# A two-layer trunk step on one core: the gate projections of two branches by Strassen's scheme

## The chip, the cores and the metric

The kernel runs on one core of one Trainium2 chip. The metric is the device time of one execution in microseconds (us), the median of several runs. Everything is 32-bit floating point. A core has TensorE for matmuls (PE in the profile, with PEld for its weight loads), VectorE (DVE), ScalarE (ACT), GpSimd (POOL), and SyncE (SP), which here only issues DMA transfers.

## The reference

Two layers run one after the other over 640 tokens: 512 latent tokens of a sample and 128 context tokens of a prompt. What matters here of each layer is this:

```python
h = rmsnorm(x, lw['g_norm1']) * (1.0 + sc1) + sh1
(qa, ka, va, qb, kb, vb, zb, ab, bb, qc, kc, vc, ga, gb, gc) = split_cols(h @ lw['w_in'])
...
merged = (jax.nn.sigmoid(ga) * (oa @ lw['w_br_a'])
          + jax.nn.sigmoid(gb) * (ob @ lw['w_br_b'])
          + jax.nn.sigmoid(gc) * (oc @ lw['w_br_c']))
x = x + gt1 * (merged @ lw['w_out'])
h2 = rmsnorm(x, lw['g_norm2']) * (1.0 + sc2) + sh2
x = x + gt2 * expert_choice_ffn(h2, lw['w_router'], lw['w_e_gate'], lw['w_e_up'], lw['w_e_down'])
```

`h` is 640 x 1024. The queries, keys and values `qa` to `vc` are 512 wide each; the gates `ga`, `gb`, `gc` are 1024 wide each. The shifts, scales and gates `sh1` to `gt2` come from a product of the condition with `w_ada` (1024 x 6144). Branch a is differential attention, branch b a bidirectional gated DeltaNet over five tiles of 128 tokens, branch c neighbourhood attention. The feed-forward part has 16 experts.

## The kernel before, in words

Weights stream from HBM in chunks of 2 MB (1024 rows by 512 columns) through a ring of three SBUF slots, `ring`, in the order of the list `PLAN`. SyncE loads a chunk when the chunk that had its slot has been used. `h` lies turned in `hT`, features on the partitions, as 8 blocks of 640 tokens. A chunk of `w_in` gives 512 output columns in five units. A unit is one PSUM bank of 512 columns, and two banks, `unit0` and `unit1`, alternate: TensorE may begin unit n when ScalarE has emptied unit n-2 (`begin`, waiting on `unit_emptied`). For a chunk with features on the partitions (`fill_rows`) the first unit holds the prompt tokens (32 matmuls of 128 columns, L988) and the other four hold 128 features by 512 sample tokens each (8 matmuls of 512 columns, L997). `fill_tokens` does it for `va` and `vc` (L1009). ScalarE copies a unit into one of eight stage buffers in `xT`, whose content lies in HBM meanwhile, and SyncE stores it to `spill`; when a branch needs it, SyncE loads it back. Four of the units of `qa` and of `ka` are rotated by VectorE before GpSimd stores them.

Each layer begins with four condition chunks (`ada`) and the chunks `qb`, `kb`, `vb`, `zb` of the DeltaNet branch. The DeltaNet is a chain of small products on TensorE with VectorE and ScalarE between them. TensorE fills the time of this chain with other work: the generator `filler` gives the matmuls of all chunks in `FILL` (condition chunks 4 to 11, `va`, `kc`, `qc`, `vc`, `qa`, `ka`, `ga` twice, `gb` twice), and `fill(gap)` takes a fixed number of calls from it at each place of the table `GAPS`: ("kv", 3) and ("kv", 4) beside the last keys and values, ("pp", t) beside the key products, "inverse" beside VectorE's inversion, (p, 0) to (p, 5) in the five rounds p of the state recurrence, and ("o", h) beside the turning of its output. A call is one matmul of 512 columns or four of 128. ScalarE's `drain(gap)` empties the units that end in a gap, in the same order. A condition chunk is two calls; behind every fourth one stands a `fold`, four small matmuls on what ScalarE has copied from the sum of the four chunks.

The gaps of one round are bounded by these lines of TensorE: L1171 (state products, behind the gap of the round before), L1179 and L1185 (behind gap 0), L1194 three times (behind gaps 1, 2 and 3), L1200 and L1204 (behind gap 4). After the five rounds come gap ("o", 4), four times L1214 and L1215 with the other ("o", h), L1134 and L1137 (turning keys), and then attention (L1242, L1254 and on). The third gate `gc` is computed beside attention (`late_units`, L1025 and L1028). Its two chunks are loaded behind `gb`. At the end of the recurrence ScalarE squares the output (`square_out`, L1780), takes roots (L1799), and only then drains ("o", 4). GpSimd issues small loads: tiles of the inversion (L779), the rotated stores (L804), caches (L814, L815) and attention biases (L828), which it then masks (L849, L854).

Of the kernel before, what the change touches and what calls it, by code (L numbers as in the profile page):

```python
# [28 lines left out]
P = 128  # L29
# [7 lines left out]
H = 4  # L37
# [28 lines left out]
UNITS_OF = dict(ada=0, fm=5, tm=5, br=5, late=0)  # L66
LATE = [("gc", 0), ("gc", 1)]
BRANCHES = "bca"
FILL = []
_a = 4  # L70
for _s in [("va", 0), ("kc", 0), ("qc", 0), ("vc", 0), ("qa", 0), ("ka", 0)] + [("g" + b, i) for b in "ab" for i in (0, 1)]:
    if _a < 12:
        FILL += [("ada", _a), _s] + [("fold", _a)] * (_a % 4 == 3)
        _a += 1
    else:
        FILL += [_s]
SPILLED = [_f for _f in FILL if _f[0] not in ("ada", "fold")]
PLAN = [("ada", a) for a in range(4)] + [("qb", 0), ("kb", 0), ("vb", 0), ("zb", 0)]
# [4 lines left out]
def kind_of(name):  # L83
    return "ada" if name == "ada" else "late" if name == "gc" else "tm" if name in ("va", "vc") else "br" if name.startswith("br") else "fm"
# [33 lines left out]
MSLOTS = (0, 3, 1, 2, 4, 5)  # L118
MRING = len(MSLOTS)
assert PRE_CHUNKS % RING == 0 and NMOE % MRING == 0  # L120


def slot_of(c):

    l, q = c // LAYER_CHUNKS, c % LAYER_CHUNKS
    if q < PRE_CHUNKS:
        return q % RING, l * (PRE_CHUNKS // RING + NMOE // MRING) + q // RING + 1
    s, n = MSLOTS[(q - PRE_CHUNKS) % MRING], (q - PRE_CHUNKS) // MRING + 1
    if s >= RING:
        return s, l * (NMOE // MRING) + n  # L130
    return s, (l + 1) * (PRE_CHUNKS // RING) + l * (NMOE // MRING) + n


def slot_before(c):

    l, q = c // LAYER_CHUNKS, c % LAYER_CHUNKS
    if q < RING:
        return l * LAYER_CHUNKS - MRING + MSLOTS.index(q)
    if q < PRE_CHUNKS:
        return c - RING  # L140
    if q < PRE_CHUNKS + MRING:
        return l * LAYER_CHUNKS + PRE_CHUNKS - RING + MSLOTS[q - PRE_CHUNKS]
    return c - MRING
# [87 lines left out]
STEPS = (9, 8, 8, 8, 8, 8)  # L231
GAPS = {("kv", 3): 3, ("kv", 4): 3} | {("pp", _t): 11 for _t in range(5)} | {"inverse": 90}
GAPS |= {(_i, _j): _q for _i in range(5) for _j, _q in enumerate(STEPS)}
GAPS |= {("o", _h): 8 if _h == 4 else 3 for _h in (4, 0, 1, 2, 3)}


def fill_units():

    units = []
    for name, i in FILL:  # L240
        if name == "ada":
            units.append((name, i, 0, 2))
        elif name == "fold":
            units.append((name, i, 0, 1))
        else:
            units += [(name, i, j, 8) for j in range(5)]
    return units
# [2401 lines left out]
```

## Time and profile before

| | us |
|---|---|
| median of 3 runs (3076.04 to 3077.58) | 3077.04 |
| the profiled execution's own time | 3078.97 |
| its span, first to last instruction | 3077.1 |
| TensorE busy, of the span | 3011.0 |
| VectorE busy | 1239.2 |
| ScalarE busy | 603.7 |
| GpSimd busy | 234.4 |

The granted TensorE clock was 0.993 of full speed over the span. The profiled execution took 1.9 us longer than the median and its span is 1.9 us shorter than its own time. A layer's part before its experts takes about 1000 us in the first layer (0 to 1000) and in the second (from about 1500). The experts take the rest. [...]

### The profile page before, as it was taken

The numbers are of one execution on the slowest core, as the hardware profiler recorded it, in microseconds if no ns is written. First come the engines' busy times: TensorE is split into PE (matmuls) and PEld (weight loads), VectorE is DVE, ScalarE is ACT, GpSimd is POOL, SyncE is SP. The second block draws the span as 40 slices with busy tenths as digits, with TensorE's granted clock in tenths as the row PEclk, the third lists the DMA queues.
The fourth block names the chain that finished last, engine by engine and source line by source line (L and its number), as shares of the span: only waits on it lengthen the run. The fifth ranks groups of instructions, "written<-read, shape, count | busy, mean of one in ns | idle before, by whom it ended". The sixth has DMA issues, their size and how long they took to land.

```text
span 3077.1 us, 49446 instructions
## 1 busy us (share of the span) xinstructions
PE 3011.0 (98%) x21834; PEld 1601.7 (52%) x21834; DVE 1239.2 (40%) x2404; ACT 603.7 (20%) x1349; POOL 234.4 (8%) x374
## 2 busy tenths in 40 slices
PE   7999999999999999999999999999999989999998
PEld 3555565656555444444455546666565454444443
DVE  4459553365354121221254694532644342112113
ACT  3241001144423000000032400011534230000001
POOL 0011000021001000000100100000110010000000
PEclk9999999999999999999999999999999989999999
DMA  6235432432343999999941552434224349999996
GB/s 269 97 130 191 155 146 97 140 123 74 133 157 125 408 398 397 403 399 396 373 176 55 187 199 93 151 118 144 93 74 145 142 174 410 395 405 400 395 403 269
DMA packets 102294, 695.55 MB, mean 226 GB/s; under 512 B 11786, under 2 KB 25142, under 8 KB 66752
## 3 DMA queue, kind: packets, MB, share of 16 engines
q1 hardware_dynamic: 75296, 613.97, 50.6%
q0 software_dynamic: 20736, 62.80, 7.0%
q10 hardware_dynamic: 6048, 15.62, 1.4%
q8 instruction: 172, 2.82, 0.4%
q14 instruction: 42, 0.34, 0.0%
HBM read 618.66 MB, written 73.68 MB: 225 GB/s over the span
## 4 chain that ended last, share of the span: by engine, by line
PE 95%; ACT 3%; DMA 1%; DVE 1%; issue 1%; DVEq 0%; POOLq 0%
PE unit L1523 14%; PE unit L997 14%; PE unit L951 12%; PE work L1526 11%; PE work L1523 7%; PE unit L1009 4%; PE unit L988 4%; PE unit L1028 4%; PE unit L1381 4%; PE unit L941 3%; PE work L965 1%; PE work L1171 1%; PE work L1194 1%; PE unit L1025 1%; DMA ring<-in_w_ada 1%; PE work L1488 1%
## 5 line engine op out<-in xcount | busy, mean ns | idle before, releaser
L997 PE MATMUL unit<-hT,ring 128*128 128x512 f32 x1024 | 452.6, 594 | 0.0
L997 PEld LDWEIGHTS unit<-hT,ring 128*128 128x128 f32 x1024 | 189.4, 190 | 217.7 <-issue 217.7
L2548 DVE SCALAR_TENSOR_TENSOR arena<-work,arena 32x256 f32<-32x256 f32 x128 | 61.7, 482 | 533.5 <-PE work L1526 532.1
L1523 PE MATMUL unit<-ring,arena 128*32 128x512 f32 x2112 | 243.4, 602 | 3.3 <-DVE arena L2536 3.3
L951 PE MATMUL unit<-hT,ring 128*128 128x512 f32 x512 | 222.2, 593 | 0.0
L1526 PE MATMUL work<-ring,arena 128*32 128x256 f32 x3072 | 183.8, 380 | 2.4 <-DVE arena L2536 2.4
L2018 ACT ACTIVATE arena<-work 128x512 f32<-128x512 f32 x32 | 19.1, 597 | 822.4 <-PE work L1541 822.4
L1629 ACT ACTIVATE xT<-unit 128x512 f32<-128x512 f32 x92 | 54.8, 596 | 590.7 <-PE unit L997 384.8
L951 PE MATMUL unit<-arena,ring 128*128 128x512 f32 x384 | 167.9, 593 | 1.6 <-ACT arena L1629 0.9
L951 PEld LDWEIGHTS unit<-hT,ring 128*128 128x128 f32 x512 | 96.2, 190 | 115.7 <-issue 115.5
L1523 PEld LDWEIGHTS unit<-ring,arena 128*32 128x32 f32 x2112 | 69.9, 111 | 149.1 <-issue 143.3
L1526 PEld LDWEIGHTS work<-ring,arena 128*32 128x32 f32 x3072 | 97.2, 110 | 92.2 <-issue 39.6
L1009 PE MATMUL unit<-ring,hT 128*128 128x512 f32 x320 | 140.7, 594 | 0.0
L988 PEld LDWEIGHTS unit<-hT,ring 128*128 128x128 f32 x1024 | 116.8, 192 | 12.4 <-issue 12.4
L1526 PE MATMUL work<-arena 128*32 128x256 f32 x2048 | 122.3, 379 | 0.0
L988 PE MATMUL unit<-hT,ring 128*128 128x128 f32 x1024 | 121.2, 277 | 0.0
L951 PEld LDWEIGHTS unit<-arena,ring 128*128 128x128 f32 x384 | 71.7, 190 | 89.1 <-issue 84.2
L1523 PE MATMUL work<-arena 128*32 128x512 f32 x1024 | 115.8, 592 | 2.1 <-ACT arena L2019 2.1
L1028 PE MATMUL unit<-hT,ring 128*128 128x512 f32 x256 | 117.0, 600 | 0.0
L2275 DVE TENSOR_TENSOR arena<-arena,work 32x512 f32<-32x512 f32 x60 | 41.0, 683 | 186.9 <-PE work L1194 186.5
L1523 PE MATMUL unit<-arena 128*32 128x512 f32 x1024 | 115.7, 592 | 0.0
L904 POOL DMA_INDIRECT moe_sum<-arena,slotu x30 | 43.2, 1440 | 941.7 <-DVE arena L2553 941.7
(447 smaller groups left out, 4201.0 us busy)
## 6 DMA issues: line engine op xcount, KB each, us to landing
ring<-in_w_e_up SPq DMA_DIRECT2D x64, 2048.0 KB, 18.5
ring<-in_w_in SPq DMA_DIRECT2D x32, 2048.0 KB, 11.6
arena<-in_w_e_gate SPq DMA_DIRECT2D x32, 2048.0 KB, 17.0
arena<-in_w_e_down SPq DMA_DIRECT2D x32, 2048.0 KB, 19.6
xT<-in_w_e_gate SPq DMA_DIRECT2D x30, 2048.0 KB, 17.1
ring<-in_w_e_down SPq DMA_DIRECT2D x30, 2048.0 KB, 17.5
ring<-in_w_ada SPq DMA_DIRECT2D x24, 2048.0 KB, 9.5
spill<-xT SPq DMA_DIRECT2D x94, 256.0 KB, 9.9
```

The costliest lines, as they stand in the source:

```text
L904: pool.indirect_dma_start(moesum[l], bass.IndirectOffsetOnAxis(token[:, s:s + 1], 0), Y[s % NROWS][0:SL, :], None, compute_op=ALU.add)\
L941: last = mm(bank[:, tile_t(m)], w[:, k, m * P:(m + 1) * P], src[:, k, TS:T], start=k == 0, stop=k == kk - 1)
L951: last = mm(bank[:, :], w[:, k, m * P:(m + 1) * P], src[:, k, 0:TS], start=k == 0, stop=k == kk - 1)
L988: last = mm(bank[:, tile_t(m)], w[:, k, m * P:(m + 1) * P], hT[:, k, TS:T], start=k == 0, stop=k == KD - 1)
L997: last = mm(bank[:, :], w[:, k, m * P:(m + 1) * P], hT[:, k, 0:TS], start=k == 0, stop=k == KD - 1)
L1009: last = mm(big[:, :], hT[:, k, tile_t(t)], w[:, k, :], start=k == 0, stop=k == KD - 1)
L1028: last = mm(ps[1][:, :], w[:, s, (j - 1) * P:j * P], hT[:, s, 0:TS], start=s == 0, stop=s == KD - 1)
L1381: last = mm(bank[:, :], wo[half][:, k, m * P:(m + 1) * P], merged[:, k, 0:TS], start=k == 0, stop=k == KD - 1)
L1523: last = mm(big[SLOTP * c:SLOTP * c + SLOTP, :], x[:, s0:s0 + SLOTP], w[:, kk, 512 * (c // 2):512 * (c // 2) + 512], start=k == 0, stop=k ...
L1526: last = mm(low[SLOTP * c:SLOTP * c + SLOTP, 0:256], xp, w[:, kk, 256 * c:256 * c + 256], start=k == 0, stop=k == KD - 1)
L1629: emptied(a_(dst, unit(n)[:, :], f, scale=scale))
L2548: STT(y[SLS:SLS + SLOTP, 256 * c:256 * c + 256], W[5][r, 0:256], gpro[r, e:e + 1], gatep[r, :], ALU.mult, ALU.mult)
```

## The change

The chunks `ga` and `gb` become a kind of their own, `fast`. In a chunk (1024 x 512), two output tiles of 128 columns, j and j+2, are one pair: the weights are a 2 x 2 of blocks A11, A12, A21, A22 (128 columns by half of the 1024 rows), and `hT` is a 2 x 2 of blocks B11, B12, B21, B22 (half of the rows by half of the 640 tokens). The four output blocks, 128 x 320 each, come from seven block products of four matmuls with 320 columns, in seven units (`fill_fast`). GpSimd makes the sums of blocks of weights before them, of `hT` once for each layer (T2, T3, T4 in ring slot 2, T1 over B12 in place), and the sums of products afterwards (`fast_sums`). ScalarE copies each product into one of two sets or a spare buffer (`copy_fast`), and SyncE stores a whole pair at once (`store_pair`). B12 is stored to HBM beforehand and loaded back when the last product that uses T1 is done, and TensorE waits for it before the late gate (`h_restored`).

The order of the fills is another one: `FILL` begins with two condition chunks, `kc` comes last of the plain ones, `vc` behind the fold of chunk 7, and each fold directly behind its condition chunk. Calls are now counted in eighths, 8 for a plain call and 5 for a matmul of 320 columns, and the credit of a gap is 8 times its number in `GAPS`. The last `gc` chunk is loaded behind `gb`, and `va` is loaded back before the last pair is stored.

```diff
+FAST = [("ga", 0), ("ga", 1), ("gb", 0), ("gb", 1)]
+FILL = [("ada", 4), ("ada", 5), ("va", 0), ("ada", 6), ("qc", 0), ("ada", 7), ("fold", 7), ("vc", 0), ("ada", 8), ("qa", 0),
+        ("ada", 9), ("ka", 0), ("ada", 10), ("kc", 0), ("ada", 11), ("fold", 11)] + FAST
-STEPS = (9, 8, 8, 8, 8, 8)
+STEPS = (8, 7, 7, 7, 8, 8)
-GAPS |= {("o", _h): 8 if _h == 4 else 3 for _h in (4, 0, 1, 2, 3)}
+GAPS |= {("o", _h): 10 if _h == 4 else 3 for _h in (4, 0, 1, 2, 3)}
...
+            if r == 1:
+                out += [("s4", g)]
+            if r == 2:
+                out += [("u2", g), ("c11", g)]
+            if r == 3 and g + 1 < NPAIRS:
+                out += [("s1", g + 1), ("s2", g + 1), ("s3", g + 1)]
+            if r == 4:
+                out += [("u3", g)]
+            if r == 5:
+                out += [("c12a", g), ("c12", g), ("c22", g)]
+            if r == 6:
+                out += [("c21", g)]
...
                 back(flat(K[0]), "ka", 0, "k_loaded")
                 back(flat(Q[0]), "qa", 0, "q_loaded")
-                store_plan(last)
+                store_pair(NPAIRS - 2)
                 sp.wait_ge(sig["q_loaded"], 16 * (2 * l + 1))
                 sp.wait_ge(sig["k_loaded"], 16 * (2 * l + 1))
                 back(flat(aV), "va", 0, "v_loaded")
+                sp.wait_ge(sig["unit_computed"], fast_unit(l, NPAIRS - 1, 3) + 1)
+                sp.dma_start(B12, hsave).then_inc(sig["h_restored"], 16)
+                load_plan(FIRST_LATE + 1)
+                store_pair(NPAIRS - 1)
...
+                    def add(out, x, y, op, task):
+                        pool.tensor_tensor(out, x, y, op).then_inc(sig["summed"], 1)
+
+                    for kind, g in TASKS[gap]:
+                        pool.wait_ge(sig["summed"], task_done(l, kind, g) - 1)
...
+                    for r, (x, y, need) in enumerate((
+                            (A11, B11, None), (A12, B21, None), (S2, T2, "s2"), (S1, B12, "s1"), (A21, T3, "s3"), (A12, B22, "s4"),
+                            (A22, T4, "t4"))):
+                        n = unit_no(l, name, i, 7 * j + r)
+                        bank = begin(n)
+                        if need and (g == 0 or need != "t4"):
+                            pe.wait_ge(sig["summed"], task_done(l, need, g))
+                        if g == 0 and r == 3:
+                            pe.wait_ge(sig["summed"], task_done(l, "t1", 0))
+                        for k in range(4):
+                            last = mm(bank[:, 0:TH], x[:, k, :], y[:, k, :], start=k == 0, stop=k == 3)
...
+                    if r == 0 and g >= 2:
+                        act.wait_ge(sig[f"stage{g % 2}_stored"], 16 * (l * STORES[g % 2] + STAGED[g % 2] + g // 2))
...
+                    elif g and r in (1, 2, 4):
+                        act.wait_ge(sig["summed"], task_done(l, {1: "c11", 2: "c12a", 4: "c21"}[r], g - 1))
```

TensorE beside the last keys and values (L1092 and, with the new line numbers, L1264), before:

```order
L1092 MATMUL work<-cst,arena 128x128 x12
L965 MATMUL work<-ring,ccol 8x512 x8
L1009 MATMUL unit0<-ring,hT 128x512
L1092 MATMUL work<-cst,arena 128x128 x12
L1009 MATMUL unit0<-ring,hT 128x512 x3
```

and now (L1113 is a condition chunk, L1157 the values `va`):

```order
L1264 MATMUL work<-cst,arena 128x128 x12
L1113 MATMUL work<-ring,ccol 8x512 x12
L1264 MATMUL work<-cst,arena 128x128 x12
L1113 MATMUL work<-ring,ccol 8x512 x4
L1157 MATMUL unit0<-ring,hT 128x512 x2
```

Half of chunk 5 has come before the second L1264 and half behind it, and `va`, whose slot is free only when `zb` is done, begins directly behind.

TensorE in round 2 at the first fast chunk (L1366 was L1194; L1113 and L1122 are condition chunk 11 and its fold; L1179 is now the product of 320 columns):

```order
L1113 MATMUL work<-ring,ccol 8x512 x4
L1366 MATMUL work<-arena 32x128 x8
L1113 MATMUL work<-ring,ccol 8x512 x4
L1122 MATMUL work<-cst,xT 128x8 x4
L1179 MATMUL unit0<-hT,ring 128x320 x4
L1179 MATMUL unit1<-hT,ring 128x320 x4
L1366 MATMUL work<-arena 32x128 x8
L1179 MATMUL unit0<-ring,xT 128x320 x4
L1179 MATMUL unit1<-hT,xT 128x320 x4
```

Two products stand between the fold and the first one that needs sums (`ring,xT`: T2 and S2).

GpSimd at the end of the recurrence (L874 is a sum, L959 and L960 were L814 and L815, L973 was L828), before only the DMAs, now:

```order
L874 TENSOR_TENSOR xT<-xT 128x320
L959 DMA arena<-in_cache_diff_k 128x512
L960 DMA arena<-in_cache_diff_v 128x512
L874 TENSOR_TENSOR xT<-xT 128x320 x4
L874 TENSOR_TENSOR ring<-ring,xT 128x4x128
L959 DMA arena<-in_cache_na_k 128x512
L960 DMA arena<-in_cache_na_v 128x512
L874 TENSOR_TENSOR xT<-xT 128x320 x7
L973 DMA arena<-rpb_scratch 16x8x32 x16
```

Five sums stand between the two cache loads and seven before the bias loads.

## Rows read from the trace of the kernel before

**Rows 1.** Page: busy us by engine, and TensorE's share in 40 slices.

```profile
PE 3011.0 (98%) x21834; PEld 1601.7 (52%) x21834; DVE 1239.2 (40%) x2404; ACT 603.7 (20%) x1349; POOL 234.4 (8%) x374
PE   7999999999999999999999999999999989999998
```

**Rows 2.** Stretches: length, busy us and instructions by engine, clock, DMA share, GB/s.

```profile
400.00:500.00 100.00, 100.00 (x548) 60.41 (x547) 49.39 (x103) 8.94 (x15) 8.04 (x15) 1.00 0.37 137
1200.00:1300.00 100.00, 100.00 (x1214) 41.29 (x1210) 19.87 (x42) 5.23 (x12) 7.06 (x6) 1.00 1.01 400
```

**Rows 3.** Groups by shape, instructions as in the page's part 5.

```profile
L1526 PE MATMUL work<-xT,arena 128*32 128x256 f32 x1024 | 61.9, 382 | 0.0
L988 PE MATMUL unit<-hT,ring 128*128 128x128 f32 x1024 | 121.2, 277 | 0.0
L997 PE MATMUL unit<-hT,ring 128*128 128x512 f32 x1024 | 452.6, 594 | 0.0
```

**Rows 4.** Stretches as rows 2, of L988, then of L997, alone.

```profile
502.70:509.00 6.30, 6.25 (x56) 6.28 (x56) 1.00 1.00 353
...
605.80:619.70 13.90, 13.82 (x32) 5.97 (x32) 1.00 0.88 301
```

**Rows 5.** Timeline of TensorE at the end of `zb`: start, length, instructions.

```profile
183.63 1.47 PE L1092 MATMUL work<-cst,arena 128*128 128x128 f32 x12
185.03 1.90 PE L965 MATMUL work<-ring,ccol 128*8 128x512 f32 x16
189.41 2.74 PE L1009 MATMUL unit<-ring,hT 128*128 128x512 f32 x6
192.58 1.16 PE L1150 MATMUL work<-arena 128*128 128x128 f32 x8 [0.43 <-ACT work L1737]
```

**Rows 6.** Timeline of SP's load behind `zb`, and its landing time.

```profile
183.82 0.33 SPq L582 DMA_DIRECT2D ring<-in_w_ada  x1
...
ring<-in_w_ada SPq DMA_DIRECT2D x1, 2048.0 KB, 7.9
```

**Rows 7.** Waits of TensorE: us in total, times, longest us.

```profile
PE work L974 <- ACT arena L1634: 0.7, 1, 0.7
PE work L965 <- ACT mod L1638: 0.8, 2, 0.4
```

**Rows 8.** GpSimd's sums of two SBUF operands: ns min/median/max.

```profile
L875 POOL TENSOR_TENSOR xT<-xT,arena x4: 1267/1270/1272, 971.9 to 2512.2; 128x512 f32<-128x512 f32 x4
L854 POOL TENSOR_TENSOR arena<-arena,cst x32: 407/417/471, 635.7 to 2280.5; 128x128 f32<-128x128 f32 x32
L849 POOL TENSOR_TENSOR arena<-arena,cst x32: 295/308/767, 635.1 to 2281.2; 128x64 f32<-128x64 f32 x32
```

**Rows 9.** Timeline of round 3 of the recurrence, VectorE and TensorE.

```profile
502.32 0.69 DVE L2257 TENSOR_TENSOR arena<-arena 128x512 f32<-128x512 f32 x1
502.93 1.28 DVE L2260 TENSOR_TENSOR arena<-work,sc 128x512 f32<-128x512 f32 x2
510.72 1.95 PE L1179 MATMUL work<-arena 128*128 128x128 f32 x16
```

**Rows 10.** Timeline of ScalarE, then of TensorE, at the recurrence's end.

```profile
611.29 0.60 ACT L1629 ACTIVATE xT<-unit 128x512 f32<-128x512 f32 x1 [9.85 <-PE unit L997]
615.16 0.22 ACT L1799 ACTIVATE sc<-sc 128x20 f32<-128x20 f32 x1
644.59 0.60 ACT L1882 ACTIVATE xT<-unit 128x512 f32<-128x512 f32 x1 [1.14 <-PE unit L1025]
...
604.09 1.95 PE L1204 MATMUL work<-arena 128*128 128x128 f32 x16
605.88 13.90 PE L997 MATMUL unit<-hT,ring 128*128 128x512 f32 x32
637.06 7.41 PE L1025 MATMUL unit<-hT,ring 128*128 128x128 f32 x64
```

**Rows 11.** Page, DMA issues: SP's stores of units, median us to landing.

```profile
spill<-xT SPq DMA_DIRECT2D x94, 256.0 KB, 9.9
```

More of the change, by code:

```diff
@@ L241, in fill_units @@
         if name == "ada":
-            units.append((name, i, 0, 2))
+            units.append((name, i, 0, 2, 8))
         elif name == "fold":
-            units.append((name, i, 0, 1))
+            units.append((name, i, 0, 1, 8))
+        elif kind_of(name) == "fast":
+            units += [(name, i, j, 4, 5) for j in range(14)]
         else:
-            units += [(name, i, j, 8) for j in range(5)]
+            units += [(name, i, j, 8, 8) for j in range(5)]
     return units
 def drains():
-    at, left, out = iter(fill_units()), 0, {}
-    unit = next(at)
-    left = unit[3]
+    pieces = [(u[:3] if k == u[3] - 1 else None, u[4]) for u in fill_units() for k in range(u[3])]
+    at, credit, out, calls = 0, 0, {}, {}
     for gap, n in GAPS.items():
-        out[gap] = []
-        for _ in range(n):
-            if unit is None:
-                break
-            left -= 1
-            if left == 0:
-                out[gap].append(unit[:3])
-                unit = next(at, None)
-                left = unit[3] if unit else 0
-    out["rest"] = ([unit[:3]] if unit else []) + [u[:3] for u in at]
-    return out
-DRAINS = drains()
+        credit, begin = credit + 8 * n, at
+        while at < len(pieces) and pieces[at][1] <= credit:
+            credit -= pieces[at][1]
+            at += 1
+        out[gap], calls[gap] = [u for u, _ in pieces[begin:at] if u], at - begin
+    out["rest"] = [u for u, _ in pieces[at:] if u]
+    return out, calls
+DRAINS, CALLS = drains()
 ROTATED = [(_n, _j) for _n in ("qa", "ka") for _j in range(1, 5)]
@@ L856, in mask_bias @@
                                     .then_inc(sig["bias_ready"], 1)
+                for h in range(H):
+                    fast_sums(("o", h))
+                fast_sums("rest")
                 load_bias(0)
@@ L1049, in filler @@
                         yield from fill_tokens(l, name, i)
+                    elif kind_of(name) == "fast":
+                        yield from fill_fast(l, name, i)
                     else:
@@ L1126, in fill @@
                 def fill(gap):
-                    for _ in range(GAPS[gap]):
+                    for _ in range(CALLS[gap]):
                         next(fills, None)
```

232 lines of the change are left out of this document (183 added, 49 removed).

## The prediction

> **What bounds the kernel now.** I read the page first: TensorE is busy in 98% of the span, and 37 of its 40 slices stand at 9 [rows 1]. Then the stretches: in 400 to 500 us, inside the recurrence, it is busy all the time at a granted clock of 1.00, VectorE half of it and GpSimd 8 us of 100; among the experts (1200 to 1300) TensorE and the DMA engines are both full [rows 2]. So work taken from TensorE before the experts is worth its full length unless a wait takes its place. The experts begin earlier by as much and last as long as before. Then I read the shapes, to price a matmul, and last the places where an instruction of the new order is followed by what waits for it.
>
> **What the products cost.** The length of an instruction with 128 rows of weights grows in a straight line: 277 ns for 128 columns, 594 ns for 512, and between them 382 ns for 256 [rows 3] (the line gives 383; that row has narrower weights). So 320 columns lie on the line. What an instruction takes from the engine is less than its length, since they overlap: 6.25 us for 56 of L988 is 0.112 us each, 13.82 us for 32 of L997 is 0.432 us each [rows 4]. The line between these gives 0.272 us for 320; I take 0.271. Bounds: it is not cheaper than 320/512 of 0.432, which is 0.270, and not dearer than 0.432.
>
> A gate chunk has 32 matmuls of 128 and 32 of 512 columns, which are 64 instructions of each: 64 x 0.112 + 64 x 0.432 = 34.8 us. Now it has two pairs of seven products of four matmuls, 112 instructions: 112 x 0.271 = 30.4 us. That is 4.4 us less for each chunk, and there are four in each of two layers: 35 us less. The other fills are the same matmuls in another order.
>
> **GpSimd's sums.** A sum of 512 columns takes 1.27 us and one of 128 takes 0.42 us [rows 8], so 2.2 ns for each further column: 0.84 us for 320 and 3.0 us for 1280. A pair needs four of 512 and seven of 320: 11.0 us, about 12 with the hand-over between chained sums, estimated at 0.1 us each (the wait of 0.7 us in [rows 7] is one copy of 0.60 us, as long as L1629's [rows 10], and 0.1 us of hand-over). TensorE needs 56 x 0.271 = 15.2 us for a pair if nothing stands between, and the recurrence does: in the trace of before the gates' place, from about 465 us to the end of the fills near 635, is 170 us; less 18 for the saving it is 152 for eight pairs, 19 us each. So GpSimd is free a third of the time, and its sums are hidden by the products.
>
> The first pair has the least room. After the last unit of `kc`, GpSimd does T3, T2, S1, S2 (3.0 + 3.0 + 1.3 + 1.3 = 8.6 us, 9.0 with hand-overs) before the third product. TensorE has a condition chunk (1.9 us [rows 5]), a fold, two products (4.3 us) and two steps of the recurrence: about 9 us with the fold's wait. T1, S3, T4 and S4 (8.5 us more) meet products four to six with as little room. I take 0.5 us a layer, with bounds 0 and 4, since one sum that is late moves all behind it.
>
> **What the shorter gaps uncover.** The gaps of a round go from 49 calls to 45, which is 3.4 us less, and no gap loses more than one call of 0.86 us. The chain behind L1171 ends on VectorE at 504.2, and TensorE comes for it at 510.7 [rows 9]: 6.5 us of room, of which the gap takes 0.9. The other steps of a round have as much, so I take nothing. The SBUF page of the Trainium skill (SBUF — State Buffer, Who interferes with whom) says that a GpSimd instruction that reads SBUF and a VectorE instruction with two SBUF inputs shut each other out for a whole instruction. That speaks against this change, and is weighed among the rivals.
>
> **What the new order costs.** (1) The slot of `va` is free when `zb` ends, at 183.8. The load at that place, of another 2 MB chunk, landed after 7.9 us [rows 6], which is 191.7. In the new order TensorE arrives at the values after two condition chunks (1.9 us each from 185.03) and one turning (1.4 us), at 190.2, and needs two calls, 1.8 us, before the key products. So these start at about 193.6 and not at 192.6, where TensorE also had waited 0.43 us [rows 5]: 1.0 us a layer; bounds 0 and 3.
> (2) A fold directly behind its chunk waits for ScalarE's copy. This occurs once in the trace, at the head of the kernel: 0.7 us [rows 7]. Two folds a layer do so now: 1.4 us a layer. The wait of the chunk behind a fold, 0.4 us and once a layer [rows 7], goes. Together 1.0 us a layer.
> (3) In gap ("o", 4) ScalarE squares and takes roots first; between its drain at 611.29 and the end of the root at 615.38 are 4.1 us [rows 10]. Two units of 3.5 us hid it. Units now last 2.2 us. Counted from 605.88, the last unit of (4, 5) ends at 6.5, ScalarE is free at 11.1, has emptied the next at 11.6, and TensorE wants that bank at 10.8: 0.8 us a layer.
> (4) The late gate needs B12 back. Its load is issued at about 21 us on the same count and TensorE asks at 31 (L1025 starts at 637.06) [rows 10]. A read of 640 KB has 10 us: nothing. `va` loaded earlier gives nothing, since it was not waited for.
> (5) The last pair: its final sum ends 2.5 us behind the last product, and its store then stands behind the 2 MB of `gc`, issued when the last product ends. With 7.9 us for that load and 1.5 for the store's own 640 KB it lands 9.5 us after the fills. ScalarE copied the first late unit at 644.59, 9.7 us after the fills [rows 10], and may now not until that store has landed. I take 0.5 us a layer, bounds 0 and 3.
> (6) Twice as many units want a prompt ScalarE (a bank must be empty after 2.2 us and not 3.5 to 7), also while it waits for sums or stores: 0.7 us a layer, bounds 0 and 6.
>
> Sum for a layer: 17.5 - 0.5 - 1.0 - 1.0 - 0.8 - 0.5 - 0.7 = 13.0 us, and 26 us for both. Against the profiled execution this is 3079.0 - 26 = 3053 us. That execution took 1.9 us longer than the median, so for the median: 3077 - 26 = **3051 us**. Without any wait it would be 3042; with all the bounds at their far ends at once the waits are 2 x 18 us and the time 3078.
>
> **Rivals.**
> A. The banks. If each fast unit ended up waiting for ScalarE, which waits in order for sums (units 1, 2 and 4 of a pair), for the store of the pair before the last (unit 0) and for its own part of the recurrence, the cost is (6) at its end and (5) with it: a store took 9.9 us to land [rows 11], mostly behind a 2 MB load, and two of them in a layer that miss by 3 us give 3051 + 12 = 3063 us. For it: ScalarE had one drain for 7 us of TensorE and now has one for 2.2. Against: by my count the store of pair 5 has some 6 us of room before pair 7.
> B. GpSimd becomes the pace. If each of its 11 sums of a pair waits for one VectorE instruction of 0.69 us [rows 9], a pair takes 12 + 7.6 = 19.6 us against 19, in the dense stretch behind round 4 against 15 to 17; with the first pair's chain late by four of them (2.8 us) this is some 5 us a layer, 3061 us. [...] For B: one of L849's sums took 767 ns against a median of 308 [rows 8]. Against: VectorE is busy half the time and less in rounds 3 and 4, and much of that reads PSUM.
> C. Slower than before. The same contention, with GpSimd's sums taking 1.7 times their priced length or more. A pair of 12 us may grow to 19 unnoticed. Beyond that each microsecond costs 8 in a layer; the gain of 13 us a layer is gone at 20.6 us a pair. At the ratio of that worst row, 767 to 308, a pair takes 27 to 30 us, and the kernel is slower by 8 x 2 x 9 less 26, about 120 us; at twice the length, 24 us a pair, it is slower by 54: 3131 us. It decides at 1.7. Against: L875 and L854 hold their lengths within 5 and 64 ns over 36 instructions.
> D. The saving isn't there: 320 columns cost more than the line says. At 0.309 us an instruction a chunk costs 34.6 us again, and the kernel would be at about 3086. The row of 256 columns, on the line within a nanosecond, speaks against it.
>
> **How the numbers follow.** Forecast 65% (3043 to 3058), A 15%, B 11%, C 5%, D 2%, and 2% for something not seen. The range is 3042 to 3067: it takes the floor without waits, the forecast's own, A and B. A run can hardly tell less than 0.2% here, 6 us. Faster by more than that (under 3070.9) in the forecast, in A and B nearly always: 0.89. Within it: the tails of A and B and the gentle part of C, 0.05. Slower: C and D, 0.06.
>
> **What would show it.** The product's row should have 896 instructions (8 chunks of 112) with a length of 434 ns, and 0.27 us from one to the next. L997 and L988 should have half their counts. TensorE's wait for the first chunk of `va` should be 1 to 2 us in each layer, and each fold's 0.7. GpSimd should be busy some 200 us more, its sums 1.27, 0.84 and 3.0 us long. Waits of the products for sums beyond 2 us a layer would speak for B, waits for ScalarE's emptying beyond 2 us a layer for A. The forecast is wrong if the span shrinks by less than 15 or more than 35 us, or if a stretch among the experts changes its length.

## The result and the profile after

The changed kernel takes 3051.11 us (median of 4 runs, 3049.69 to 3054.68), beside 3077.31 us for the kernel before on the same chip: a ratio of 0.9914, 95% interval 0.9900 to 0.9929. That is 26.2 us less. The forecast was 3051, with a range of 3042 to 3067. Two later sets of runs of the same kernel gave 3050.77 and 3049.83 us.

Where a line of before has moved, the new number is given with it. The page of the changed kernel, busy us by engine and TensorE's slices [rows 1]:

```profile
PE 2976.9 (98%) x21706; PEld 1615.5 (53%) x21706; DVE 1260.3 (41%) x2404; ACT 628.3 (21%) x1421; POOL 444.3 (15%) x558
PE   7999999999998999999999999999999989999998
```

TensorE has 128 instructions fewer and is busy for 34.1 us less. The span shrank by 24.2 us, so 10 us more of it is idle; most of that is the new waits below. GpSimd is busy for 210 us more, VectorE for 21. The same stretches as in [rows 2] (length, busy us and instructions of PE, PEld, DVE, ACT, POOL, clock, DMA share, GB/s):

```profile
400.00:500.00 100.00, 99.22 (x549) 66.54 (x548) 47.39 (x87) 11.26 (x23) 42.69 (x38) 1.00 0.32 115
1200.00:1300.00 100.00, 100.00 (x1222) 41.55 (x1215) 19.89 (x42) 5.23 (x12) 7.98 (x7) 1.00 1.01 401
```

The experts are as they were. In the recurrence one wait of 0.78 us has come in, and GpSimd is busy for 43% and not 8%. The products and the sums by shape (duration in ns, min/median/max), which answer to [rows 3] and [rows 8]:

```profile
L1179 PE MATMUL unit<-hT,ring x384: 432/432/537, 460.1 to 2131.6; 128*128 128x320 f32 x192
L1179 PE MATMUL unit<-ring x256: 432/432/537, 470.0 to 2133.7; 128*128 128x320 f32 x128
L874 POOL TENSOR_TENSOR xT<-xT x112: 849/859/1410, 473.1 to 2136.4; 128x320 f32<-128x320 f32 x112
L874 POOL TENSOR_TENSOR xT<-xT,ring x16: 1262/1266/1600, 463.2 to 2109.5; 128x512 f32<-128x512 f32 x16
L874 POOL TENSOR_TENSOR ring<-ring,hT x2: 2876/2878/2879, 458.9 to 1972.7; 128x1280 f32<-128x1280 f32 x2
```

With the two forms not shown (128 of `ring,xT`, 128 of `hT,xT`) these are 896 instructions of products, two for each of the 8 chunks' 56 matmuls. How far one stands from the next is read from the timeline of TensorE in pair 1, whose products follow each other directly:

```profile
473.34 2.32 PE L1179 MATMUL unit<-hT,ring 128*128 128x320 f32 x8
475.49 2.32 PE L1179 MATMUL unit<-ring 128*128 128x320 f32 x8
477.64 2.32 PE L1179 MATMUL unit<-hT,ring 128*128 128x320 f32 x8
```

Eight take 2.15 us from start to start, 0.269 us each, against 0.271 forecast. The waits of TensorE (us in total, times, longest us) in the whole run, those that are new or have grown:

```profile
PE work L1652 <- DMA arena<-h_rows,slotu: 3.3, 2, 1.6
PE work L1122 <- ACT xT L1807: 3.1, 4, 0.8
PE work L1386 <- DVE arena L2502: 2.4, 2, 1.2
...
PE unit L1157 <- DMA ring<-in_w_in: 2.3, 2, 1.2
```

L1157 (before L1009) and L1122 (before L974, [rows 7]) are the waits of terms (1) and (2). L1386 and L1652 were not in the prediction. No row names a product that waits for GpSimd.

Because a kernel's instructions on TensorE stand in a fixed order, the start of the same instruction in two runs says what has been won up to there. Starts in the changed kernel less those in the kernel before, us (each is the first instruction of its line in the stretch, read from the two timelines; the last two rows are the group of products that ends the experts' turns, before and behind it):

| place (line before) | layer 1 | layer 2 |
|---|---|---|
| last keys and values (L1092) | +0.4 | -10.9 |
| key products (L1150) | +1.3 | -10.0 |
| round 0 (L1171) | +2.1 | -9.2 |
| round 1 | -2.1 | -13.3 |
| round 2 | -5.5 | -16.7 |
| round 3 | -9.4 | -20.6 |
| round 4 | -13.2 | -24.5 |
| norm (L1214) | -13.3 | -24.5 |
| attention (L1242) | -14.5 | -25.7 |
| first expert (L1479) | -12.8 | -26.2 |
| expert turns, all 16 | -12.2 | -25.7 |
| behind the last expert | -10.7 | -24.2 |

From its own start up to attention layer 1 gains 14.5 us and layer 2 15.0 (2.1 us are lost up to round 0 of layer 1 and the rest won behind it). The experts take as long as before, to 0.01 us over all 16. But 3.8 us are given back between attention and the next layer in layer 1, and 1.5 in layer 2. Of this, 1.5 us in each layer is one group of products behind the last turn. The kernel before, then the changed one (start, length), and the changed one's clock there (the third value from the end):

```profile
1517.20 3.64 PE L1523 MATMUL work<-arena 128*32 128x512 f32 x32 [1.05 <-ACT arena L2019]
```
```profile
1505.04 5.12 PE L1696 MATMUL work<-arena 128*32 128x512 f32 x32 [1.05 <-ACT arena L2214]
```
```profile
1504.00:1508.00 4.00, 2.96 (x16) 0.92 (x20) 0.00 (x0) 0.87 (x2) 4.00 (x9) 0.58 0.96 339
```

The granted clock fell to about half there, and at 3020 us again. In layer 1, 1.6 us more are the wait L1652 for the first gathered rows.

### The profile page after: what moved, and what is told of

Read it like the earlier page. It is cut to its first block, busy times and chain, and to the rows that moved or that the text cites. A ratio compares the mean times of both kernels' runs of the same rounds, so it can differ in the third digit from the quotient of the medians.

```text
span 3052.9 us, 49631 instructions
## 1 busy us (share of the span) xinstructions
PE 2976.9 (98%) x21706; PEld 1615.5 (53%) x21706; DVE 1260.3 (41%) x2404; ACT 628.3 (21%) x1421; POOL 444.3 (15%) x558
## 4 chain that ended last, share of the span: by engine, by line
PE 94%; ACT 2%; DMA 2%; DVE 1%; issue 1%; ACTq 0%; DVEq 0%; POOLq 0%
PE unit L1696 14%; PE unit L1099 12%; PE work L1699 11%; PE unit L1179 7%; PE work L1696 7%; PE unit L1145 7%; PE unit L1157 5%; PE unit L1198 4%; PE unit L1554 4%; PE unit L1089 3%; PE unit L1136 2%; PE work L1343 1%; PE work L1113 1%; PE work L1366 1%; PE unit L1195 1%; DMA ring<-in_w_ada 1%
## 5 line engine op out<-in xcount | busy, mean ns | idle before, releaser
L1145 PE MATMUL unit<-hT,ring 128*128 128x512 f32 x512 | 225.3, 593 | 0.0
L1099 PE MATMUL unit<-hT,ring 128*128 128x512 f32 x512 | 222.2, 592 | 0.0
L1099 PE MATMUL unit<-arena,ring 128*128 128x512 f32 x384 | 167.9, 593 | 1.6 <-ACT arena L1802 0.9
L1099 PEld LDWEIGHTS unit<-hT,ring 128*128 128x128 f32 x512 | 96.2, 190 | 115.8 <-issue 115.5
L1145 PEld LDWEIGHTS unit<-hT,ring 128*128 128x128 f32 x512 | 95.0, 190 | 109.3 <-issue 109.3
L1157 PE MATMUL unit<-ring,hT 128*128 128x512 f32 x320 | 139.7, 593 | 2.3 <-DMA ring<-in_w_in 2.3
L1198 PE MATMUL unit<-hT,ring 128*128 128x512 f32 x256 | 117.0, 600 | 0.0
L1179 PE MATMUL unit<-hT,ring 128*128 128x320 f32 x384 | 111.6, 435 | 0.2
L874 POOL TENSOR_TENSOR xT<-xT 128x320 f32<-128x320 f32 x112 | 101.7, 908 | 62.5 <-ACT xT L1875 56.4
L1554 PE MATMUL unit<-arena,ring 128*128 128x512 f32 x256 | 110.7, 593 | 0.0
L1696 PE MATMUL work<-ring,arena 128*32 128x512 f32 x960 | 108.5, 592 | 0.0
```

The source lines that it names most:

```text
L874: pool.tensor_tensor(out, x, y, op).then_inc(sig["summed"], 1)
L1099: last = mm(bank[:, :], w[:, k, m * P:(m + 1) * P], src[:, k, 0:TS], start=k == 0, stop=k == kk - 1)
L1145: last = mm(bank[:, :], w[:, k, m * P:(m + 1) * P], hT[:, k, 0:TS], start=k == 0, stop=k == KD - 1)
L1157: last = mm(big[:, :], hT[:, k, tile_t(t)], w[:, k, :], start=k == 0, stop=k == KD - 1)
L1179: last = mm(bank[:, 0:TH], x[:, k, :], y[:, k, :], start=k == 0, stop=k == 3)
L1198: last = mm(ps[1][:, :], w[:, s, (j - 1) * P:j * P], hT[:, s, 0:TS], start=s == 0, stop=s == KD - 1)
```

## The experiments

Medians in us; each ratio is against the kernel before in the same set of runs.

| run | median (range) | ratio, 95% interval |
|---|---|---|
| changed_again | 3050.77 (3049.97 to 3052.7) | 0.9907 (0.9892 to 0.9922) |
| order_alone | 3082.15 (3081.01 to 3083.89) | 1.0010 (1.0001 to 1.0019) |
| sums_8_columns | 3046.3 (3045.43 to 3048.7) | 0.9893 (0.9877 to 0.9908) |
| sums_twice | 3144.22 (3141.3 to 3145.9) | 1.0212 (1.0196 to 1.0227) |
| four_sums_twice | 3057.99 (3055.28 to 3061.46) | 0.9929 (0.9915 to 0.9942) |
| folds_later | 3054.33 (3051.83 to 3055.22) | 0.9917 (0.9904 to 0.9931) |
| sums_after_norm | 3044.64 (3043.94 to 3045.39) | 0.9886 (0.9871 to 0.9902) |
| folds_and_sums | 3047.6 (3044.25 to 3048.68) | 0.9897 (0.9882 to 0.9913) |
| norm_repeat | 3046.29 (3043.61 to 3048.15) | 0.9889 (0.9873 to 0.9906) |
| fold7_and_norm | 3045.4 (3041.85 to 3047.09) | 0.9885 (0.9869 to 0.9902) |
| changed_third | 3049.83 (3048.27 to 3051.84) | 0.9903 (0.9887 to 0.9920) |

**The changed kernel again** (no edit).

> The changed kernel once more, beside the others on one chip. Theory (products shorter by an eighth, waits of 4 to 5 us a layer given back): 26 us under the kernel before. Rival (part of the gain is chance of the run): under 20 or over 32. In the profile of the changed kernel one group at the end of each layer's experts took 5.1 us where it took 3.6 before; if that is a matter of the run and not of the change, it is missing or elsewhere in this one.

It repeats the first result within 0.4 us, and the rows L1122, L1157 and L1386 within 0.3 us. The table of starts is the same to 0.5 us up to attention of layer 1. Behind it the two profiles differ by where the clock falls: here the long group behind the experts stands in layer 2 alone, and two others have come in, at 950 and 2462 us (below).

**The order of the fills alone.** The kernel before, with the changed kernel's list and plain gate chunks.

```diff
-FILL = []
-_a = 4
-for _s in [("va", 0), ("kc", 0), ("qc", 0), ("vc", 0), ("qa", 0), ("ka", 0)] + [("g" + b, i) for b in "ab" for i in (0, 1)]:
...
+FILL = [("ada", 4), ("ada", 5), ("va", 0), ("ada", 6), ("qc", 0), ("ada", 7), ("fold", 7), ("vc", 0), ("ada", 8), ("qa", 0),
+        ("ada", 9), ("ka", 0), ("ada", 10), ("kc", 0), ("ada", 11), ("fold", 11), ("ga", 0), ("ga", 1), ("gb", 0), ("gb", 1)]
```

> The kernel before with the new order of the fills (two condition chunks first, folds directly behind their chunks, kc last) and plain gates; no Strassen products. Theory: the order costs by itself what the trace of the changed kernel shows at these places, a wait of 1.1 us for the first va chunk (of which 0.4 us was there before in another wait) and two folds with 0.8 us, less the 0.4 us wait that goes: some 2 us a layer, 4 us slower than before (3081). Then the products alone gave about 30 us. Rival (the order pays for itself by steadier loads, and the products gave only 20): 5 us faster than before.

It loses 2.4 us in the median against 3079.73, where 4 had been expected, and its profiled span is 3.3 us longer. Its waits:

```profile
PE work L968 <- ACT xT L1628: 3.1, 4, 0.8
PE unit L1003 <- DMA ring<-in_w_in: 2.5, 2, 1.3
```

These are the rows L1122 and L1157 of the changed kernel, to 0.2 us: both waits belong to the order of the fills and not to the products. Attention starts 1.6 us late in layer 1, and 14.5 us early in the changed kernel. So the products with all that belongs to them bring 16.1 us up to there, and over the whole run 31.4 us by the medians of this set (3082.15 less 3050.77).

**Sums of 8 columns.** GpSimd adds 8 columns and not 320 to 1280; what the products are made from and give is wrong for the rest.

```diff
+                        out, x, y = [v[:, :, 0:2] if len(v.shape) == 3 else v[:, 0:8] for v in (out, x, y)]
                         pool.tensor_tensor(out, x, y, op).then_inc(sig["summed"], 1)
```

> The changed kernel with each of GpSimd's sums cut to 8 columns, so that the output is not the reference's: what remains of the sums is their order and their waits. Theory (the sums are hidden, except where they lock VectorE out at the norm of the recurrence's output): 2 to 3 us faster than the changed kernel, since the wait of 1.2 us a layer behind the norm goes; VectorE's lines with two SBUF operands fall back to 0.69 us. Rival (GpSimd sets the pace, rival B of the prediction): 8 us faster or more.

The starts of L1171 differ from those of changed_again by 0.14 or 0.15 us in all ten rounds, and by the same in each. Before the end of round 4, nothing is won by sums of almost no length: they are hidden entirely. Behind it TensorE's first product with the norm (L1386) starts 1.4 us earlier in each layer, because its wait is gone. That is 2.8 us; the median is 4.5 us lower, more than the 2 to 3 expected. The mean granted clock of the profiled execution, 0.993 against 0.992, goes that way. This points to VectorE's norm, L2502 (L2307 before, L2503 here). First the kernel before, then the changed kernel, then this one (durations in ns, min/median/max):

```profile
L2307 DVE TENSOR_TENSOR arena<-arena,sc x10: 681/682/691, 615.7 to 2143.2; 128x512 f32<-128x512 f32 x10
```
```profile
L2502 DVE TENSOR_TENSOR arena<-arena,sc x10: 693/1345/1354, 600.5 to 2118.7; 128x512 f32<-128x512 f32 x10
```
```profile
L2503 DVE TENSOR_TENSOR arena<-arena,sc x10: 682/683/693, 600.1 to 2114.6; 128x512 f32<-128x512 f32 x10
```

And the place itself in the changed kernel, VectorE, then GpSimd, then TensorE (start, length):

```profile
600.51 5.77 DVE L2502 TENSOR_TENSOR arena<-arena,sc 128x512 f32<-128x512 f32 x5
...
600.64 5.08 POOL L874 TENSOR_TENSOR xT<-xT 128x320 f32<-128x320 f32 x4 [0.31 <-ACT xT L1875]
605.80 1.60 POOL L874 TENSOR_TENSOR ring<-ring,xT 128x512 f32<-128x512 f32 x1
...
606.33 0.65 PE L1386 MATMUL work<-cst,arena 128*128 128x128 f32 x4 [1.22 <-DVE arena L2502]
```

Four sums and five norm products, all with both operands in SBUF, take turns: 4 x 0.86 + 3.1 is 6.5 us of work apart, and together they end after about 5.8. In the steady turn a sum and a product start every 1.27 us; alone, sums start every 0.93 us and products every 0.62, which makes 1.55. So each holds the other up for most of its length, though not all. The four sums took 1.19 to 1.28 us each and not 0.86, and the products 1.22 in the mean and not 0.69. VectorE's L2486, of the same 512 columns but with one input in PSUM, kept its 680 ns in the recurrence beside the sums (676 to 681, against 672 to 680 before). The Trainium skill (SBUF — State Buffer, Who interferes with whom) says that a VectorE instruction with two SBUF inputs contends with a GpSimd instruction that reads SBUF, for ports held by an exclusive lock, and that one with at most one SBUF input, outside its 2-port modes, does not. For the norm and for L2486 the trace agrees.

The norm isn't the only line that the sums slow. In the recurrence L2490 (L2295 before), both inputs in SBUF, took up to 1948 ns where 692 was the longest before, and a VectorE copy inside SBUF, with one input, took up to 1333. The copy in the kernel before, in the changed one and in this one:

```profile
L2221 DVE COPY arena<-arena x8: 216/217/223, 484.1 to 541.8; 32x128 f32<-32x128 f32 x8
```
```profile
L2416 DVE COPY arena<-arena x8: 215/575/1333, 475.4 to 529.2; 32x128 f32<-32x128 f32 x8
```
```profile
L2417 DVE COPY arena<-arena x8: 214/218/223, 475.0 to 528.8; 32x128 f32<-32x128 f32 x8
```

No row of TensorE's waits names these lines, and the starts of the rounds show that they cost nothing.

**All sums of a pair twice.** Each sum but T1 to T4 is made twice. S3, S4 and sums behind the products stand in place, so the values of the gates are others.

```diff
-                        pool.tensor_tensor(out, x, y, op).then_inc(sig["summed"], 1)
+                        if kind[0] != "t":
+                            pool.tensor_tensor(out, x, y, op).then_inc(sig["summed"], 1)
+                            pool.wait_ge(sig["summed"], task_done(l, kind, g) - 1)
+                            pool.tensor_tensor(out, x, y, op).then_inc(sig["summed"], 1)
+                        else:
+                            pool.tensor_tensor(out, x, y, op).then_inc(sig["summed"], 2)
...
```

> The changed kernel with each of GpSimd's sums but T1 to T4 done twice, one after the other, so that the output is not the reference's. A pair's sums then take about 24.5 us, and TensorE has 20 us for a pair. Theory (they are hidden up to a pair's time and set the pace beyond it, the point at which rival C of the prediction decides): 4.5 x 8 x 2 = 72 us and a few more for the first pair, 70 to 85 us slower than the changed kernel, so some 50 us slower than before. Rival (each sum only delays its own product and most have room): under 20 us slower than the changed kernel.

This is rival C made real. It is 64.5 us slower than the kernel before, where the rival's price for 24 us a pair was 54, and 93 us slower than the changed kernel, beyond the 70 to 85 expected. TensorE's waits:

```profile
PE unit L1184 <- POOL ring L877: 47.4, 16, 5.6
...
PE unit L1184 <- ACT xT L1880: 12.4, 10, 3.3
```

In layer 1 round 3 starts 5.5 us late against the changed kernel, round 4 19, the norm 37 and attention 47: GpSimd, once behind, is the pace to the end of the fills. L2507, the norm here, took 1751 ns in the median. The waits of L1184, with 3.4 us in a row not shown, are 63 us. The clock would cover most of the other 30: the profiled execution's mean granted clock was 0.983, and 0.992 in changed_again. As an estimate from these two, 1.7% of 3140.9 us less 0.8% of 3050.9 is 29 us of clock more that was not granted.

**Only the four sums ahead of the products twice,** in pairs 1 to 7. S3 and S4 stand in place, and so come out as other values, contrary to what the expectation says of the result.

```diff
-                        pool.tensor_tensor(out, x, y, op).then_inc(sig["summed"], 1)
+                        if g and kind[0] == "s":
+                            pool.tensor_tensor(out, x, y, op).then_inc(sig["summed"], 1)
+                            pool.wait_ge(sig["summed"], task_done(l, kind, g) - 1)
+                            pool.tensor_tensor(out, x, y, op).then_inc(sig["summed"], 1)
+                        else:
+                            pool.tensor_tensor(out, x, y, op).then_inc(sig["summed"], 2)
...
```

> The changed kernel, except that GpSimd makes the four sums of 512 columns that stand ahead of the products (S1 to S4) of pairs 1 to 7 twice each, one behind the other with the same result; the rest of the computation is whole. It adds 4 x 1.27 + 4 x 0.07 = 5.4 us to a pair, which was measured at about 12 us by the rows of the changed kernel: 17.4 us a pair. Theory (a pair of sums may grow to the 19 to 20 us that the recurrence gives a pair of products, and is free below it): in the rounds nothing, and 0 to 4 us over the changed kernel in all, since the last pairs lie behind round 4, where a pair of products has only 15 to 17 us: 3050 to 3055 us. Rival (each microsecond of GpSimd costs its share, as in the run with all sums of a pair twice, +93 us for about 12 us more a pair): 5.4/12 x 93 = 42 us more, 3093 us. What tells them apart: the starts of L1171 in the five rounds against those of the changed kernel, and the wait of L1184 (the product) for GpSimd, 63 us over both layers in the other run, a few us here by the theory.

The rival that each microsecond of GpSimd costs is dead (3058, not 3093). The waits of TensorE between 440 and 680 us:

```profile
PE work L1391 <- DVE arena L2507: 2.7, 1, 2.7
PE work L1127 <- ACT xT L1812: 0.8, 1, 0.8
PE work L1431 <- ACT arena L2046: 0.7, 2, 0.4
PE unit L1445 <- DVE arena L2590: 0.7, 1, 0.7
```

No product waits for GpSimd at 17.4 us a pair. From round 0 to round 4 TensorE loses 0.4 us a layer against changed_again. The norm's wait is 2.7 us and not 1.2, while more sums fall beside it. The median is 7 us above the changed kernel, 3 more than the theory allowed, and its runs spread by 6 us. In the profiled execution 3.2 us are the norm's waits (5.5 us in both layers against 2.3). TensorE's clock right behind that wait in layer 1 (the third value from the end):

```profile
607.00:610.50 3.50, 3.43 (x10) 2.65 (x11) 1.03 (x3) 0.00 (x0) 3.21 (x4) 0.52 0.16 64
```

Half of 3.5 us is some 1.7 us more, an estimate. The wait for `va` (L1162) grew too, to 3.6 us over both layers against 2.3 to 2.6; why isn't known.

**Folds later.** The fold of chunk 7 behind `vc`, that of chunk 11 behind the first fast chunk.

```diff
-("ada", 7), ("fold", 7), ("vc", 0), ... ("ada", 11), ("fold", 11)] + FAST
+("ada", 7), ("vc", 0), ("fold", 7), ... ("ada", 11), FAST[0], ("fold", 11)] + FAST[1:]
```

> The changed kernel, with the fold of chunk 7 moved behind vc and the fold of chunk 11 behind the first fast chunk. All of the computation is whole. Theory (a fold directly behind its chunk waits 0.7 to 0.8 us for ScalarE's copy, the row L1122 <- ACT, 3.1 us in 4; the chunk that comes next does not wait then): two folds in each of two layers, 3.1 us over both less 0 to 1.0 for the wait of the bank behind them, 2 to 3 us less: 3048 us where the changed kernel is 3050.8. Rival (other waits close up behind it, since the fold's place in the recurrence gave VectorE and ScalarE that time): no difference. The row of waits L1122 <- ACT should be gone by both; the starts of L1171 in rounds 0 to 2 against those of the changed kernel tell them apart.

The wait is gone as expected, and nothing is won: 3054.33 us, 3.6 above the 3050.8 of changed_again where 2 to 3 less had been expected. Another wait stands in its place:

```profile
PE unit L1179 <- POOL xT L874: 3.4, 2, 1.7
```

TensorE and GpSimd at the first pair, in this kernel (start, length):

```profile
457.75 4.58 PE L1179 MATMUL unit<-hT,ring 128*128 128x320 f32 x16
464.01 0.78 PE L1179 MATMUL unit<-ring,xT 128*128 128x320 f32 x2 [1.69 <-POOL xT L874]
...
455.30 2.91 POOL L874 TENSOR_TENSOR ring<-hT 128x1280 f32<-128x1280 f32 x1 [23.57 <-PE unit L1145]
458.29 2.89 POOL L874 TENSOR_TENSOR ring<-ring,hT 128x1280 f32<-128x1280 f32 x1
461.26 1.27 POOL L874 TENSOR_TENSOR xT<-ring 128x512 f32<-128x512 f32 x1
462.61 1.26 POOL L874 TENSOR_TENSOR xT<-xT,ring 128x512 f32<-128x512 f32 x1
```

T3, T2, S1 and S2 end at 463.9, and the third product has been waiting for them. In the changed kernel (the first profile) S2 ended at 464.4 and the product started at 465.6: 1.2 us of room, which the fold (0.8 us of wait and 0.9 of work) had made. At the start of round 3 of layer 1 this kernel is 0.9 us behind changed_again. The fold of chunk 7 did give something: at the start of round 2 it was 0.3 us ahead, 0.5 us more than at the key products.

**Sums behind the norm.** One wait more on GpSimd, ahead of the sums of gap ("o", 4).

```diff
                     if i:
+                        pool.wait_ge(sig["otok_ready"], l + 1)
                         fast_sums(("o", 4))
```

> The changed kernel, with one wait more: in the stretch behind the last round GpSimd begins the sums of gap (o, 4) only when VectorE has normed the output of the recurrence (otok_ready). All of the computation is whole. Theory (the five norm products on VectorE, L2502, both inputs in SBUF, take 1.22 us each and not 0.69 while GpSimd adds beside them; TensorE waits 1.2 us a layer for the last of them at L1386): L2502 back to 0.69 us, the wait L1386 <- L2502 of 2.3 us in 2 gone, and 2 to 2.5 us less, 3048.4 us where the changed kernel is 3050.8. Rival 1 (the length of L2502 has another cause, as its place beside ScalarE or a DMA): L2502 stays at 1.2 us and nothing is gained. Rival 2 (the sums are then late for their products): L2502 is short, but the wait of the products L1179 for GpSimd appears and the time is 0 to 5 us longer.

L2503 is the norm here:

```profile
L2503 DVE TENSOR_TENSOR arena<-arena,sc x10: 684/685/693, 600.4 to 2111.5; 128x512 f32<-128x512 f32 x10
```

It takes 0.69 us, TensorE doesn't wait at L1387, no product waits for GpSimd, and the starts gain 1.4 us at the norm of each layer. So theory and mechanism hold. The median is 6.1 us under that of changed_again (another set of runs), more than the 2.8 that the starts explain.

**Both edits.** The two diffs above together.

> Both of the last two edits on the changed kernel: the folds of chunks 7 and 11 later, and the sums of gap (o, 4) behind VectorE's norm. All of the computation is whole. Theory (the two waits lie at different places of TensorE's stream and add): 4 to 5.5 us less than the changed kernel, about 3046 us. Rival (the chain from the recurrence to attention has one slack that both would use): no more than the better of the two alone, 3048 us.

3047.6 us: no better than the sums alone. Its row "PE unit L1180 <- POOL xT L874: 3.3, 2, 1.7" is the wait of folds_later. The edits don't add: the later fold of chunk 11 brings its wait along. The rival (no more than the better of the two) came true.

**The sums behind the norm again** (no further edit), **with the fold of chunk 7 alone**, and **the changed kernel a third time**, on one chip. The diff of the middle one, against sums_after_norm:

```diff
-("ada", 7), ("fold", 7), ("vc", 0)
+("ada", 7), ("vc", 0), ("fold", 7)
```

> The same kernel as sums_after_norm (the changed kernel, in which GpSimd begins the sums of gap (o, 4) only when VectorE has normed the output), beside the changed kernel on the same chip. All of the computation is whole. The wait that it takes away is 2.3 us over both layers, but the first run came out about 6 us under the changed kernel in the median and at a mean granted clock of 0.994 where that had 0.992; two groups of L1566 in the stretch before routing (at 950 and 2462 us) took 1.6 us longer in the changed kernel and not in this one. Theory 1 (these steps of the clock belong to a kernel, since they come at the same places in each of its runs): again 0.994, the two groups of normal length, 5 to 7 us under the changed kernel. Theory 2 (they are chance of the run or the chip): the clock as in the changed kernel, 2 to 3 us under it.

> The same with the fold of chunk 7 alone moved behind vc. All of the computation is whole. The two folds together gave nothing: at the start of round 2 TensorE was 0.5 us earlier, by the fold of chunk 7, and behind round 2 it was 1.3 us later, since the product that needs T2 and S2 came before them (a wait of 1.7 us for GpSimd). Theory: the fold of chunk 7 alone gives 0.5 us a layer with no wait for GpSimd at the first pair, 1 us less than the run beside it; too little for the medians to show, so it is read from the starts of L1171 and the rows of waits. Rival (every microsecond won ahead of the first pair is lost at T2, as GpSimd's chain starts from the last unit of kc, which comes earlier too): then no difference at round 2 either.

> The changed kernel itself, beside the other two on the same chip: 3049 to 3053 us, mean granted clock 0.991 or 0.992, with the wait L1386 <- L2502 of 2.3 us in 2. Theory 1 (the clock's steps belong to a kernel): the groups of L1566 at 950 and 2462 us again 1.5 us longer. Theory 2 (chance): not so in this run, or in the other two as well.

3046.29, 3045.4 and 3049.83 us. The fold of chunk 7 alone wins what was expected of it: from the first key product to round 3 TensorE gains 11.15 us on the kernel before in each layer, where changed_third and norm_repeat gain 10.65; and no product waits for GpSimd. In the median, 0.9 us is inside the spread of the runs. The clock's steps keep to no kernel at either of the two places. Windows of the changed_again kernel, then of sums_after_norm over the same instructions (the granted clock is the third value from the end):

```profile
947.00:950.00 3.00, 3.00 (x29) 2.90 (x25) 0.18 (x1) 1.49 (x3) 0.89 (x1) 0.95 0.00 0
950.00:953.00 3.00, 3.00 (x15) 3.00 (x15) 1.51 (x7) 1.11 (x3) 1.95 (x3) 0.50 0.00 0
953.00:956.00 3.00, 3.00 (x29) 2.92 (x28) 0.28 (x1) 0.00 (x0) 0.00 (x0) 0.98 0.00 0
```
```profile
948.50:951.50 3.00, 3.00 (x28) 3.00 (x28) 1.51 (x7) 1.32 (x3) 2.16 (x3) 1.00 0.00 0
```

In changed_again 32 instructions of L1566 run there mostly at 0.50 of full speed, the 1.2 GHz level, and take 5.35 us and not 3.82, right behind a stretch of matmuls of one and 16 columns, through which TensorE was busy. So it was in changed_again and changed_third, not in the first run of the changed kernel (1.00 from 949 to 957), and in neither run of the sums behind the norm. But fold7_and_norm and folds_and_sums, which have the sums behind the norm too, had it (0.57 from 947 to 951, 0.66 from 947 to 952). At 2462 us all three profiles of the changed kernel had it, norm_repeat too, and the other three with the sums behind the norm not. Such a step is 1.5 us. The mean clock leans to the kernel all the same: 0.991 or 0.992 in 10 of the changed kernel's 12 repeats and 0.993 in two, 0.993 or 0.994 in 15 of the 16 repeats of the four runs with the sums behind the norm and 0.992 in one. Neither theory of the two holds alone, and what makes the clock fall here stays open.

The version that beats both kernels is thus the one with the sums behind the norm: 3.5 us under the changed kernel in the set that they share and 6.1 us under that of another set, 33 to 36 under the kernel before. The starts at the norm explain 2.8 us of this, and the mean clocks lean the same way. Adding the fold of chunk 7 costs nothing and wins 0.5 us a layer by the starts.

## Why the prediction was right

- **Products, 17.5 us a layer: right.** 896 instructions, 0.269 us apart. A gate chunk's 32 matmuls of 512 columns are 64 instructions (L997: 1024 in 16 such chunks), as reckoned, and the line through the rows of 128 and 512 columns gave 320 within 1%. order_alone, with the same order and plain gates, shows that the gain is theirs.
- **GpSimd hides its sums: right.** Lengths were 0.859, 1.27 and 2.9 us against 0.84, 1.27 and 3.0, and the hand-over 0.07 us against 0.1. A pair needs 11.9 us. sums_8_columns shows a cost of nothing in the rounds, four_sums_twice no wait of a product at 17.4 us, and sums_twice, at twice the sums, waits for them all through the last rounds. So the point from which they decide lies between 17.4 and about 24 us; the 20.6 us of rival C lies within it.
- **The first pair, 0.5 us: it was 0.** The room was 1.2 us, and folds_later shows how narrow that is.
- **(1) The late load of `va`, 1.0 us: right.** The wait at L1157 was 1.1 and 1.2 us, and in order_alone 1.2 and 1.3. From the last keys and values to the key products TensorE loses 0.9 us in layer 1 and 1.0 in layer 2.
- **(2) The folds, 1.0 us: right** as a wait (0.78 us each, four times), and it is the price of the order alone. But they aren't all to be had back: moving the fold of chunk 7 wins 0.5 us a layer, and the other covers T2 and S2.
- **(3) ScalarE in gap ("o", 4), 0.8 us: the size was near and the cause was wrong.** A product waited 0.2 us for ScalarE's emptying there, and not 0.8. TensorE lost 1.2 us a layer just behind it to VectorE's norm, which GpSimd's four sums had slowed. Rival B named this very lock, priced it for every sum, and put it at 5 us a layer. It is real and slows VectorE in the rounds too, but costs time only where it meets what TensorE waits for, one place a layer.
- **(5) The last pair's store, 0.5 us: the wait came and cost nothing.** ScalarE waited 2.9 us for the store at 631.7, and from attention's start to L1242's end TensorE's lead stayed at 14.4 to 14.5 us.
- **(6) Prompt ScalarE, 0.7 us: 0.1 us a layer,** and 0.4 at most at one place (changed_third), though the gates' units went from 20 to 56 a layer and not to twice as many. Rival A is dead with it.
- **The sum.** The terms with their measured sizes are 17.5 - 1.6 (L1157, and both folds less the waits that went) - 1.2 - 0.2 = 14.5 us a layer, near the 14.5 and 15.0 that the starts show, where I had 13.0. Over both layers that is 29 and not 26 us. The 3 us too few were met by 3 us lost behind attention, of which the prediction had said nothing but that the experts keep their length. They do, but the wait for the first gathered rows (L1652, L1479 before) went from 0.6 to 3.3 us, and the clock fell at other places: the mean granted clock of the profiled executions was 0.993 before and 0.991 after. As an estimate, 0.9% of 3052.9 us less 0.7% of 3077.1 is 6 us more of clock that was not granted, where this profile gave back 5.3 us in all. Why the clock fell more is open. So part of the agreement with 3051 is luck: up to attention the products less the order are worth 29 us.

The first gather's wait was between 0.3 and 3.3 us over the runs with no edit near it, and its cause was not looked for.

## What to carry to other kernels

Work moved to an idle engine is free up to the pace of what it feeds, and then costs its full excess; work that pace out first, in us per repeat, and test it by doubling. Here the waits were 63 us of the 93 that doubling cost, and a lower granted clock would cover most of the rest. An idle helper can still slow its neighbour when they work side by side: look at the one or two instructions of the neighbour that the bound engine waits for, and start the helper's work behind them. And before a wait is removed, ask what it was covering: here the fold's 0.8 us hid a chain that ended 1.2 us ahead of its need.

## What was not expected of the hardware

- GpSimd's float sums with both operands in SBUF cost 0.86 us for 320 columns, 1.27 for 512 and 2.9 for 1280, and a chain of them with a semaphore between costs only 0.07 us each on top.
- Beside VectorE's two-operand SBUF products both slow down: 0.86 to about 1.2 and 0.69 to 1.22 us; a VectorE instruction with a PSUM input kept 0.68 us beside such sums, and a VectorE copy inside SBUF went from 0.22 us to between 0.22 and 1.33.
- The granted clock fell to 0.50 for 3 us behind a few small matmuls although TensorE was busy throughout (947 to 953 above), at a cost of 1.5 us, and in other runs of the same kernel it did not fall there.
